# A hybrid encoder trunk on one core: four of the gate and branch blocks formed by seven half-size products in place of eight

## The chip, the cores and the metric

The kernel runs on one core of one Trainium2 chip. The metric is the device time of one execution in microseconds (us), input and output transfers of the launch left out. The engines are TensorE (PE in the profile, PEld its weight loads), VectorE (DVE), ScalarE (ACT), GpSimd (POOL) and SyncE (SP, here the queue that issues nearly all loads of weights).

## The reference

Two layers; all data are float32. SEQ is 256 rows (two row tiles of 128, called tt below), D is 1024. Each layer is a mixer and then a mixture of experts (MoE):

```python
h = modulate(rms_norm(x, norm1_g[i]), sh1, sc1)
proj = h @ w_in[i]                                   # (256,1024) @ (1024,6656)
u_hy, q, k, v, gate_hy, gate_at = jnp.split(proj, split_idx, axis=-1)
y_hy = hyena_mixer(u_hy, ...)                        # (256,768)
y_at = dilated_attention_mixer(rope(q), rope(k), v)  # (256,256)
merged = (sigmoid(gate_hy) * (y_hy @ w_br_h[i])      # (256,768) @ (768,1024)
          + sigmoid(gate_at) * (y_at @ w_br_a[i]))   # (256,256) @ (256,1024)
x = x + g1[:, None, :] * (merged @ w_out[i])
h = modulate(rms_norm(x, norm2_g[i]), sh2, sc2)
x = x + g2[:, None, :] * grouped_moe(h, ...)         # 16 experts, 3 matrices of 1024x512 each
```

gate_hy and gate_at are each 1024 columns of `proj`: four column blocks of W = 512, called gate blocks 0 to 3 here. `y_hy @ w_br_h` has two column blocks of 512, called branch blocks 0 and 1.

## The kernel before

All five engines have a program of their own, written out in order; semaphores (`p_...` counted by PE, `v_...` by DVE, `a_...` by ACT) are the only thing that orders one engine against another. PE's order in a layer is: projections of `h`, the convolution, attention (eight units, with gate blocks 0 and 1 woven in), then the stage that the change touches, the product with `w_out`, the router, and the MoE in seven steps.

The stage begins behind the last attention unit. `branch(q, w, src, ks, o)` forms one column block of a branch: for each row tile `ks` matmuls with 128 rows of `src` as weights and 512 columns of `w` moving, into bank 2 or 3. Branch blocks 0 and 1 take x0T (y_hy transposed, six chunks of 128 rows) and `w_br_h`. `gate(q, tt, half)` does the same for gate blocks from hT (eight chunks) and `w_in`, into bank 7 or 4; blocks 2 and 3 stand behind the branch blocks. Then `branch(2)` and `branch(3)` take the attention's part (two chunks). ACT opens the gates (Sigmoid, `open_gate`), DVE multiplies (L1868, L1871) and adds (L1872) into `merged`, whose transposes (L1083) PE does next.

In layer 0 DVE also forms, between its other work, the sums of the next layer's modulation: `next_sums(n, n+1)` is eight scaled additions `ada_part` of 512 columns each over a 2 MB block of `w_ada`, four blocks in all (L1586, L1588, L1590). `ada_post(n, L + 1)` on PE, eight instructions in the trace, folds each finished block and stands between the branch and gate blocks. In layer 1 there are none of these.

Weights pass through a ring of six buffers of 2 MB (two halves each) and, for the MoE, some further half buffers in idle memory: TABLE (in cst), EXTRA to EXTRA + 3 (in `wide`), ROWS and TAIL (in area). `place_blocks` plans the slots, `released` says which semaphore frees each, and SP issues the loads strictly in that order, so one load that waits for its slot holds all behind it. EXTRA to EXTRA + 2 lie where the convolution keeps its tables, and before the change are free once branch block 1 is done.

Of the kernel before, what the change touches and what calls it, by code (L numbers as in the profile page):

```python
# [14 lines left out]
P = 128  # L15
# [53 lines left out]
RING = 6  # L69
EXTRA = 2 * RING  # L70
# [114 lines left out]
def trunk_kernel(nc, t, out):  # L185
    with ExitStack() as ctx:
# [111 lines left out]
        mtmp = region(W)  # L298

# [97 lines left out]
        p_c = sem("p_c")  # L397
        v_c = sem("v_c")
        a_c = sem("a_c")
        p_vec = sem("p_vec")  # L400
        p_hv = sem("p_hv")
# [5 lines left out]
        v_A2 = sem("v_A2")  # L407
# [36 lines left out]
        p_br = sem("p_br")  # L444
        v_br = sem("v_br")
# [5 lines left out]
        p_sh = sem("p_sh")  # L451
# [6 lines left out]
        v_lg = sem("v_lg")  # L458
        a_xn = sem("a_xn")
        p_lg = sem("p_lg")  # L460
        a_lg = sem("a_lg")
        v_oh = sem("v_oh")
# [55 lines left out]
        def place_blocks():  # L518
            landings = [0] * len(halves)
            free = [(u, None) for u in range(EXTRA)]  # L520
            for key in loads:
                L, kind, b, half = key
                if kind == "moe":
                    if (b, half) == ((0, 0, 0), 0):
                        free = [(u, None) for u in (TABLE, EXTRA, EXTRA + 1, EXTRA + 2)]\
                            + [f for f in free if f[0] < EXTRA] + [(EXTRA + 3, None)]
                        if L + 1 == DEPTH:
                            free.insert(12, (ROWS, None))
# [24 lines left out]
        def released(L, kind, b, half):  # L553
# [5 lines left out]
            if kind == "in":  # L559
                if b < 4:  # L560
                    return p_u, L * NSC + 4 * b + 4
                if b < 7:
                    return p_qk, L * 6 + 2 * b - 7
                return (p_v, L * 3 + (1, 3)[b - 7]) if b < IN_A else (p_gate, L * 8 + 2 * (b - IN_A) + 2)
            if kind == "brh":
                return p_br, L * 8 + 2 * b + 2
            if kind == "bra":
                return p_br, L * 8 + 8
# [52 lines left out]
        def _(sp):  # L621
# [7 lines left out]
            for L, kind, b, half in loads:  # L629
                _, u, _, olds = plan[L, kind, b, half]  # L630
                dst, landing, _ = slot(L, kind, b, half)
                for old in olds:
# [3 lines left out]
                    elif u == TABLE:  # L636
                        sp.wait_ge(p_br, L * 8 + 1)
                    elif u == ROWS:
                        sp.wait_ge(p_br, L * 8 + 8)
# [40 lines left out]
        def _(pool):  # L680
# [15 lines left out]
            for L in range(DEPTH):  # L696
# [20 lines left out]
                if L + 1 < DEPTH:  # L717
                    pool.wait_ge(p_lg, L + 1)
# [14 lines left out]
        def _(pe):  # L733
# [11 lines left out]
            for L in range(DEPTH):  # L745
# [80 lines left out]
                if L == 0:  # L826
                    pe.wait_ge(s_id, 16)
                    pe.wait_ge(s_mlp, 16 * N_MLP)
                    pe.transpose(bank[4][:, 0:4], hrow, ident[0:4, 0:4]).then_inc(p_hv, 1)
# [4 lines left out]
                    pe.transpose(bank[0][:, 0:ND], crow, ident[0:ND, 0:ND]).then_inc(p_c, 1)  # L834
# [20 lines left out]
                    for l in range(DEPTH):  # L855
                        pe.transpose(bank[6][:, l * P:l * P + R_ALL], vrows[l][:, :], ident[0:R_ALL, 0:R_ALL])
                    pe.transpose(bank[6][:, DEPTH * P:DEPTH * P + DEPTH * 6 * ND], brow[:, :],
                                 ident[0:DEPTH * 6 * ND, 0:DEPTH * 6 * ND]).then_inc(p_vec, 1)
# [163 lines left out]
                def gate(q, tt, half):  # L1022
                    w = block_of("in", IN_A + q)
                    if q >= 1 and half == 0:
                        pe.wait_ge(a_gate, L * 8 + 2 * q + tt - 1)
# [14 lines left out]
                for u in range(UNITS):  # L1040
# [5 lines left out]
                    if u == 5:  # L1046
                        pe.wait_ge(v_sh, 2 * L + 2)
                        pe.wait_ge(v_mod, (L + 1) * 4)
                        mm(bank[1][:, 0:NE], ones, shift_sum, True, True).then_inc(p_sh, 1)
                if L + 1 < DEPTH:  # L1050
                    ada_post(0, L + 1)

                def branch(q, w, src, ks, o):
                    for tt in range(NT):
                        if q >= 1:
                            pe.wait_ge(v_br, L * 8 + 2 * q + tt - 1)
                        for k in range(ks):
                            last = mm(bank[2 + tt][:, :], src[:, k, tt * P:(tt + 1) * P], w[:, k, o:o + W],
# [3 lines left out]
                for q in range(2):  # L1062
                    wv = landed("brh", q)[:, 0:NH_CH * W].rearrange("p (k f) -> p k f", f=W)
                    branch(q, wv, x0T, NH_CH, 0)
                    if L + 1 < DEPTH:
                        ada_post(1 + q, L + 1)
                for q in (2, 3):
                    for tt in range(NT):
                        gate(q, tt, 0)
                        gate(q, tt, 1)  # L1070
                        if L + 1 < DEPTH and (q, tt) == (2, 1):
                            ada_post(3, L + 1)
                wv = landed("bra", 0)[:, 0:2 * D].rearrange("p (k f) -> p k f", f=D)
                pe.wait_ge(a_yat, L + 1)
                branch(2, wv, yatT, 2, 0)
                branch(3, wv, yatT, 2, W)
# [53 lines left out]
                last.then_inc(p_lg, 1)  # L1130
# [3 lines left out]
                pe.wait_ge(v_oh, L + 1)  # L1134
# [98 lines left out]
                pe.wait_ge(a_xn, L + 1)  # L1233
# [68 lines left out]
        def _(sc):  # L1302
# [7 lines left out]
            sc.wait_ge(p_c, 1)  # L1310
            sc.activation(stat[:, 0, 0:ND], bank[0][:, 0:ND], ACT.Sigmoid).then_inc(a_c, 1)

            for L in range(DEPTH):
# [68 lines left out]

                def open_gate(q, tt):
                    if q >= 2:
                        sc.wait_ge(v_br, L * 8 + 2 * (q - 2) + tt + 1)
                    sc.wait_ge(p_gate, L * 8 + 2 * q + tt + 1)
# [21 lines left out]
                for q in (2, 3):  # L1408
                    for tt in range(NT):
                        open_gate(q, tt)  # L1410
# [34 lines left out]
                sc.wait_ge(v_lg, L + 1)  # L1445
                sc.activation(rt[score], rt[logit], ACT.Sigmoid).then_inc(a_lg, 1)
# [4 lines left out]
                last.then_inc(a_xn, 1)  # L1451
# [91 lines left out]
        def _(dv):  # L1543
# [22 lines left out]
            for L in range(DEPTH):  # L1566
# [105 lines left out]
                if L == 0:  # L1672
                    dv.wait_ge(p_hv, 1)
# [16 lines left out]
                    dv.wait_ge(p_vec, 1)  # L1690
# [48 lines left out]
                def second_shift_and_scale():  # L1739
# [4 lines left out]
                    dv.scalar_tensor_tensor(A2[:, :], modT[:, 4 * ND:5 * ND], 1.0, n2[:, L, :],  # L1744
                                            ALU.add, ALU.mult).then_inc(v_A2, 1)
                    dv.wait_ge(v_A2, L + 1)
# [93 lines left out]
                ada_parts(N_LATE, 0, 2 * ND)  # L1840
                ada_gate(N_LATE)
                ada_gate(N_LATE + 1)

                def next_sums(first, stop):
                    for n in range(first, stop if L + 1 < DEPTH else first):
                        for k in range(ND):
                            ada_part(n, k, L + 1, "next")

                next_sums(0, 1)
                dv.wait_ge(p_sh, L + 1)  # L1850
                link(dv.tensor_copy(shift_logit, bank[1][:, 0:NE]))
                next_sums(1, 2)
                for q in range(4):
# [297 lines left out]
```

## Time and profile before

| | |
|---|---|
| three runs, median (lowest to highest) | 1084.14 us (1083.87 to 1084.25) |
| the profiled execution | 1084.34 us, span 1082.6 us |
| mean granted clock of PE | 0.994 |
| PE busy / PEld / DVE / ACT | 97% / 53% / 43% / 16% of the span |
| stage of the change, layer 0 | from 243.66 us of the span |
| stage of the change, layer 1 | from 758.98 us of the span |
| MoE, layer 0 / layer 1 | from 343.76 / 856.42 us |
| moved from memory | 332.78 MB, mean 307 GB/s |

The span runs from the first to the last instruction. A float32 matmul shows as two PE instructions in the trace and as one in the program order, so a count in the trace is twice the number of matmuls. A merged row of PE gives the start, the time to the modelled end of its last matmul (which overlaps the next row) and the count; the pace is read from start to start.

### The profile page before, as it was taken

The page shows a single profiled execution, that of the slowest core. Times are in us where ns is not written, and L with a number is a line of the kernel's source. Part 1 is how long each engine was busy: PE and PEld are TensorE (multiplying, and loading weights), DVE is VectorE, ACT ScalarE, POOL GpSimd, SP SyncE. Part 2 cuts the span into 40 slices and gives each one's busy share as a digit, 9 for nine tenths or more (in the row PEclk, how much of TensorE's full clock was granted, in tenths as well). Part 3 has the DMA queues.
Part 4 walks back from the last instruction along what each step waited for, and adds up shares of the span by engine and source line. Part 5 has one row for each costly group of instructions (what it writes and reads, how often), then busy time and mean ns, then how long its engine had stood idle before and what let it go on. Part 6 is the DMA issues. An engine that isn't in the chain of part 4 may idle for free.

```text
span 1082.6 us, 17591 instructions
## 1 busy us (share of the span) xinstructions
PE 1048.1 (97%) x7533; PEld 574.6 (53%) x7533; DVE 469.6 (43%) x1024; ACT 174.3 (16%) x340; POOL 20.4 (2%) x40
## 2 busy tenths in 40 slices
PE   7999999999999999999999999999999999999895
PEld 4788667654446344433448866765444634444231
DVE  3477696644125422351335779660102532222223
ACT  4121101310014113101121110031001411111002
POOL 3000000000000000000000000000000000000000
PEclk9999999999999999999999999999999999999898
DMA  9996846268963999999999884525665399999993
GB/s 314 391 386 250 305 157 212 82 215 320 414 233 133 407 420 413 423 420 420 421 400 377 301 299 169 181 94 194 245 266 226 127 420 423 420 421 420 421 421 135
DMA packets 90917, 332.78 MB, mean 307 GB/s; under 512 B 5020, under 2 KB 5355, under 8 KB 66005
## 3 DMA queue, kind: packets, MB, share of 16 engines
q1 hardware_dynamic: 87905, 323.56, 76.6%
q0 software_dynamic: 2048, 6.09, 1.6%
q10 hardware_dynamic: 884, 1.97, 0.6%
q8 instruction: 61, 1.00, 0.4%
q14 instruction: 19, 0.16, 0.0%
HBM read 330.54 MB, written 1.05 MB: 306 GB/s over the span
## 4 chain that ended last, share of the span: by engine, by line
PE 87%; DVE 6%; DMA 3%; SPq 1%; issue 1%; ACT 1%; DVEq 0%
PE bank L735 84%; DMA ring<-in_moe_w_dram 3%; SPq L665 1%; PE bank L1175 1%; PE bank L1007 1%; DVE wide L1588 0%; DVE area L1781 0%; DVE wide L1786 0%; DVE area L1784 0%; PE bank L1093 0%; DVE area L1782 0%; DVE area L1783 0%; PE bank L788 0%; DVE wide L1785 0%; DVE area L1659 0%
## 5 line engine op out<-in xcount | busy, mean ns | idle before, releaser
L735 PE MATMUL bank<-ring,hT 128*32 128x512 f32 (+3 forms) x1808 | 313.1, 557 | 1.7 <-issue 1.7
L735 PE MATMUL bank<-hT,ring 128*32 128x256 f32 (+1 forms) x2112 | 214.1, 380 | 0.2 <-DVE hT L1622 0.2
L735 PEld LDWEIGHTS bank<-ring,hT 128*32 128x32 f32 (+2 forms) x1808 | 128.8, 136 | 150.0 <-issue 146.3
L735 PEld LDWEIGHTS bank<-hT,ring 128*32 128x32 f32 (+1 forms) x2112 | 158.9, 132 | 55.1 <-issue 8.7
L735 PE MATMUL bank<-area 32*64 32x64 f32 (+5 forms) x648 | 96.1, 363 | 0.5 <-ACT area L1470 0.5
L735 PE MATMUL bank<-ring,area 128*32 128x512 f32 x664 | 81.9, 594 | 0.5 <-ACT area L1470 0.5
L735 PEld LDWEIGHTS bank<-area 32*64 32x64 f32 (+4 forms) x648 | 43.8, 145 | 54.2 <-issue 52.2
L2055 DVE TENSOR_TENSOR area<-bank,area 128x512 f32<-128x512 f32 x14 | 9.7, 692 | 130.2 <-PE bank L735 130.2
L735 PE MATMUL bank<-wide,hT 128*32 128x512 f32 x368 | 65.8, 603 | 0.0
L1588 DVE SCALAR_TENSOR_TENSOR area<-ring,wide,area 128x512 f32<-128x512 f32 x84 | 63.1, 751 | 2.5
L735 PE MATMUL bank<-ring,wide 128*128 128x512 f32 (+1 forms) x192 | 64.0, 597 | 0.0
L735 PE MATMUL bank<-ring,xn 128*128 128x512 f32 x128 | 55.6, 592 | 0.0
L2066 DVE TENSOR_TENSOR area<-bank,g2b 128x512 f32<-128x512 f32 x28 | 19.4, 692 | 79.2 <-PE bank L735 79.2
L735 PE MATMUL bank<-area,xn 128*128 128x128 f32 x448 | 52.5, 275 | 0.1
L735 PEld LDWEIGHTS bank<-area,xn 128*128 128x128 f32 x448 | 51.1, 192 | 0.4 <-issue 0.4
L1985 DVE TENSOR_TENSOR x<-x,bank 128x512 f32<-128x512 f32 x56 | 38.5, 688 | 24.8 <-PE bank L735 24.8
L735 PEld LDWEIGHTS bank<-ring,area 128*32 128x32 f32 x664 | 22.3, 110 | 44.1 <-issue 42.5
L735 PEld LDWEIGHTS bank<-ring,wide 128*128 128x128 f32 (+1 forms) x192 | 25.4, 163 | 33.6 <-issue 30.5
L1971 DVE TENSOR_SCALAR hT<-bank,A,modT 128x128 f32<-128x128 f32 x56 | 19.1, 404 | 52.2 <-PE bank L735 52.2
L735 PEld LDWEIGHTS bank<-ring,xn 128*128 128x128 f32 x128 | 24.0, 190 | 28.7 <-issue 28.7
L1464 ACT ACTIVATE area<-bank 128x512 f32<-128x512 f32 x14 | 8.4, 598 | 185.4 <-PE bank L735 185.4
L735 PE MATMUL bank<-cst,hT 128*32 128x512 f32 x128 | 34.2, 622 | 2.8 <-DMA wide<-in_moe_w_dram 2.8
(266 smaller groups left out, 898.0 us busy)
## 6 DMA issues: line engine op xcount, KB each, us to landing
ring<-in_moe_w_dram SPq DMA_DIRECT2D x135, 1024.0 KB, 14.4
ring<-in_w_in_dram SPq DMA_DIRECT2D x26, 2048.0 KB, 11.3
ring<-in_w_ada_dram SPq DMA_DIRECT2D x24, 2048.0 KB, 14.1
wide<-in_moe_w_dram SPq DMA_DIRECT2D x33, 1024.0 KB, 12.5
cst<-in_moe_w_dram SPq DMA_DIRECT2D x13, 1024.0 KB, 15.0
area<-in_moe_w_dram SPq DMA_DIRECT2D x11, 1024.0 KB, 14.6
ring<-in_w_out_dram SPq DMA_DIRECT2D x4, 2048.0 KB, 7.8
ring<-in_w_br_h_dram SPq DMA_DIRECT2D x4, 1536.0 KB, 7.8
```

Source lines behind the costliest of these rows:

```text
L665: sp.dma_start(dst.rearrange("p (k f) -> p k f", f=D if m == 2 else FE), t[name][L, experts[e], :, :].rearrange(order, p=P)[:, part, :]).t ...
L735: return pe.matmul(dst, lhsT, rhs, start=start, stop=stop, skip_group_check=True)
L1007: last = pe.transpose(bank[5][:, b * P:(b + 1) * P], prob[:, u, b * P:(b + 1) * P], ident)
L1175: last = pe.transpose(bank[0][:, f * P:(f + 1) * P], act[:, f::NF], ident)
L1464: sc.activation(sil, bank[0][:, :], ACT.Silu).then_inc(a_sil, 1)
L1588: link(dv.scalar_tensor_tensor(part, wk, c, part, ALU.mult, ALU.add))
L1971: last = dv.tensor_scalar(hg[:, k, :], bank[3][:, (k - 4) * P:(k - 3) * P], A2[:, k:k + 1], modT[:, 3 * ND + k:3 * ND + k + 1], ALU.mult, ...
L1985: dv.tensor_tensor(x[:, tt, cols], x[:, tt, cols], bank[2 + 2 * tt + h][:, :], ALU.add)\
L2055: dv.tensor_tensor(act, bank[1][:, :], sil, ALU.mult).then_inc(v_act, 1)
L2066: dv.tensor_tensor(yS[:, cols], bank[6 + h][:, :], g2b[:, cols], ALU.mult).then_inc(v_yS, 1)
```

## The change

Four blocks in each layer (branch blocks 0 and 1, gate blocks 2 and 3) are formed by `seven(...)` instead of `branch` and `gate`. The block's product (256 rows by 512 columns) is cut in two by two quarters of 128 rows by 256 columns, the inner dimension in two halves of `kc` chunks (3 or 4). The eight quarter products become seven (Strassen's scheme in Winograd's form): each is `kc` matmuls of 256 columns. Their operands are sums that DVE forms: `sum_of` (of x0T or hT, four for each pair of blocks, 384 or 512 columns), `mix` (of the weights, four for each block, 768 or 1024 columns, the third in place in the ring). The results are put together by ACT, which copies products 1 and 2 out (`keep_products`), and by DVE, which forms two partial sums (`first_sums`) and three quarters (`quarter`), each 256 columns, and in blocks 0 and 1 multiplies them with the gates (`merge`). In gate blocks 2 and 3 ACT applies Sigmoid by quarters (`open_quarters`).

Product 1 of a block waits for `quarter(1)` of the block before, product 3 for its `quarter(2)`; product 4 waits for ACT's copy of product 1, product 5 for the first partial sum, product 6 for ACT's second copy, product 7 for `quarter(0)` and the last `mix`.

DVE's order is written out by hand in `block_in_seven`; the 16 remaining additions for the next layer (layer 0 only) are strewn into the four blocks as 3, 2, 4 and 7. EXTRA + 2 now holds operands of the scheme, is free only when all 28 products of the layer are done, and is moved from the fourth to the tenth place of the first MoE loads. Some semaphores are joined to free others for this.

```diff
@@ PE
+                def seven(i, w, src, sums, mixed, kc):
+                    n = L * SEVEN + i
...
+                    if i:
+                        pe.wait_ge(v_sev, n * 4 - 1)
+                    if i > 2:
+                        pe.wait_ge(a_gate, L * 12 + 5)
+                    product(X, of(0, 0), whole(0, 0), True)
+                    pe.wait_ge(v_sum, L * 8 + i // 2 * 4 + 1)
+                    pe.wait_ge(v_mix, n * 4 + 1)
+                    product(Y, summed(0), combined(0), True)
+                    if i:
+                        pe.wait_ge(v_sev, n * 4)
+                    else:
+                        pe.wait_ge(a_gate, L * 12 + 3)
+                    pe.wait_ge(v_sum, L * 8 + i // 2 * 4 + 2)
+                    pe.wait_ge(v_mix, n * 4 + 2)
+                    product(V, summed(1), combined(1), True)
+                    pe.wait_ge(a_sev, n * 2 + 1)
+                    product(X, of(1, 0), whole(1, 0), False)
...
+                    pe.wait_ge(v_sev, n * 4 + 1)
+                    product(V, summed(2), whole(0, 1), False)
...
+                    pe.wait_ge(a_sev, n * 2 + 2)
+                    product(Y, summed(3), whole(1, 1), False)
+                    pe.wait_ge(v_mix, n * 4 + 4)
+                    pe.wait_ge(v_sev, n * 4 + 2)
+                    product(V, of(1, 1), combined(2), False)
@@ DVE
+                def block_in_seven(i, parts):
+                    at = [parts[0]]
+                    def fill(n):
+                        for _ in range(min(n, parts[1] - at[0])):
+                            next_part(at[0])
+                            at[0] += 1
+                    mix(i, 3)
+                    first_sums(i)
+                    if i == 2:
+                        sum_of(2, 3)
+                    if i < 3:
+                        mix(i + 1, 0)
+                    fill(1)
+                    quarter(i, 0)
+                    if i < 3:
+                        mix(i + 1, 1)
+                    fill(2)
+                    quarter(i, 1)
+                    if i < 3:
+                        mix(i + 1, 2)
+                    if i == 1:
+                        sum_of(2, 2)
+                    fill(2)
+                    quarter(i, 2)
+                    fill(ND)
...
+                block_in_seven(0, (2 * ND, 2 * ND + 3))
+                block_in_seven(1, (2 * ND + 3, 2 * ND + 5))
+                block_in_seven(2, (2 * ND + 5, 3 * ND + 1))
+                block_in_seven(3, (3 * ND + 1, 4 * ND))
@@ SP
+                    elif u == EXTRA + 2:
+                        sp.wait_ge(p_sev, (L + 1) * SEVEN * 7)
                     elif u >= EXTRA:
-                        sp.wait_ge(p_br, L * 8 + 4)
+                        sp.wait_ge(p_sev, (L * SEVEN + 2) * 7)
```

PE, layer 0, the start of the stage (`ring` are the weights as loaded, `wide` before the change is x0T, 128x1 is `ada_post`). Before:

```order
L735 MATMUL bank<-cst,area 128x1 x4
L735 MATMUL bank<-ring,wide 128x512 x12
L735 MATMUL bank<-cst,area 128x1 x4
L735 MATMUL bank<-ring,wide 128x512 x12
L735 MATMUL bank<-cst,area 128x1 x4
L735 MATMUL bank<-ring,hT 128x512 x16
```

And with the change, where the rows that name `wide` alone take combined operands on both sides:

```order
L756 MATMUL bank<-cst,area 128x1 x4
L756 MATMUL bank<-ring,wide 128x256 x3
L756 MATMUL bank<-wide 128x256 x6
L756 MATMUL bank<-ring,wide 128x256 x9
L756 MATMUL bank<-wide 128x256 x3
L756 MATMUL bank<-cst,area 128x1 x4
L756 MATMUL bank<-ring,wide 128x256 x3
```

Each block of twelve matmuls of 512 columns is now 21 of 256; one `ada_post` is still between blocks 0 and 1, and the one that stood between blocks 1 and 2 now stands behind block 3.

DVE, layer 0, around branch block 0 (`xn` holds the opened gates). Before, from the last addition ahead of the block:

```order
L1590 SCALAR_TENSOR_TENSOR area<-ring,wide,area 128x512
L1868 TENSOR_TENSOR area<-bank,xn 128x512 x2
L1586 TENSOR_SCALAR area<-ring,wide 128x512
L1588 SCALAR_TENSOR_TENSOR area<-ring,wide,area 128x512 x6
L1590 SCALAR_TENSOR_TENSOR area<-ring,wide,area 128x512
```

With the change, from `quarter(0, 0)` to `quarter(0, 2)` (the three rows of L1991; product 1 of block 1 waits for the second of them):

```order
L1991 TENSOR_TENSOR area<-bank,area 128x256
L1983 TENSOR_TENSOR area<-area,xn 128x256
L1983 TENSOR_TENSOR area<-bank,xn 128x256
L1969 TENSOR_TENSOR wide<-ring,wide 128x768
L1674 SCALAR_TENSOR_TENSOR area<-ring,wide,area 128x512 x2
L1991 TENSOR_TENSOR area<-bank,area 128x256
L1983 TENSOR_TENSOR area<-area,xn 128x256
L1969 TENSOR_TENSOR ring<-ring 128x3x256
L1991 TENSOR_TENSOR area<-bank,area 128x256
```

Between the first quarter and the second stand two gate products, a combination of block 1's weights and two additions for the next layer.

## Rows read from the trace of the kernel before

**Rows 1.** The page, busy time, share of the span and instructions by engine.

```profile
PE 1048.1 (97%) x7533; PEld 574.6 (53%) x7533; DVE 469.6 (43%) x1024; ACT 174.3 (16%) x340; POOL 20.4 (2%) x40
```

**Rows 2.** Timeline of PE, layer 0, the stage of the change: start, us, instructions.

```profile
243.66 10.55 PE L735 MATMUL bank<-ring,wide 128*128 128x512 f32 x24
254.04 0.95 PE L735 MATMUL bank<-cst,area 128*128 128x1 f32 x8
254.85 10.55 PE L735 MATMUL bank<-ring,wide 128*128 128x512 f32 x24
...
266.04 13.98 PE L735 MATMUL bank<-ring,hT 128*128 128x512 f32 x32
...
294.49 7.19 PE L735 MATMUL bank<-ring,wide 128*128 128x512 f32 x16
```

**Rows 3.** Timeline of PE, layer 1, the same stage.

```profile
758.98 20.87 PE L735 MATMUL bank<-ring,wide 128*128 128x512 f32 x48
779.68 27.63 PE L735 MATMUL bank<-ring,hT 128*128 128x512 f32 x64
```

**Rows 4.** Timeline of PE, layer 1, projections: matmuls of 256 columns in four waited groups.

```profile
603.95 13.98 PE L735 MATMUL bank<-hT,ring 128*128 128x256 f32 x64
617.77 1.02 PE L735 MATMUL bank<-area,cst 128*128 128x512 f32 x2
```

**Rows 5.** Groups by line and shape, DVE, 60 to 1075 us: count, busy us, mean ns.

```profile
L1588 DVE SCALAR_TENSOR_TENSOR area<-ring,wide,area 128x512 f32<-128x512 f32 x84 | 63.1, 751 | 2.5
L1872 DVE TENSOR_TENSOR area<-area 128x512 f32<-128x512 f32 x8 | 5.5, 692 | 0.3
L1659 DVE TENSOR_TENSOR wide<-wide 128x1536 f32<-128x1536 f32 x2 | 3.5, 1756 | 0.0
```

**Rows 6.** Timeline of DVE, layer 0, around branch block 0.

```profile
235.91 4.69 DVE L1588 SCALAR_TENSOR_TENSOR area<-ring,wide,area 128x512 f32<-128x512 f32 x6
240.64 0.75 DVE L1590 SCALAR_TENSOR_TENSOR area<-ring,wide,area 128x512 f32<-128x512 f32 x1
249.16 0.69 DVE L1868 TENSOR_TENSOR area<-bank,xn 128x512 f32<-128x512 f32 x1 [7.77 <-PE bank L735]
254.31 0.69 DVE L1868 TENSOR_TENSOR area<-bank,xn 128x512 f32<-128x512 f32 x1 [4.46 <-PE bank L735]
254.92 0.48 DVE L1586 TENSOR_SCALAR area<-ring,wide 128x512 f32<-128x512 f32 x1
```

**Rows 7.** The chain that ended last, layer 0, behind the stage.

```profile
302.54 0.70 DVE area L1872
303.29 1.09 PE bank L1083 x8
```

**Rows 8.** The page, weight loads of 128 columns: count, busy us, mean ns.

```profile
L735 PEld LDWEIGHTS bank<-ring,xn 128*128 128x128 f32 x128 | 24.0, 190 | 28.7 <-issue 28.7
```

**Rows 9.** Timeline of SP's queue, layer 0.

```profile
266.47 3.31 SPq L665 DMA_DIRECT2D cst<-in_moe_w_dram  x1
```

**Rows 10.** Stretches of layer 1 by engine; the last three numbers are PEclk, DMA share, GB/s.

```profile
855.00:860.00 5.00, 4.96 (x44) 4.79 (x43) 1.56 (x6) 1.68 (x5) 0.00 (x0) 1.00 0.01 3
865.00:870.00 5.00, 5.00 (x52) 1.46 (x48) 4.31 (x21) 0.60 (x1) 0.00 (x0) 1.00 0.92 370
```

**Rows 11.** The chain that ended last, layer 1, MoE.

```profile
990.32 27.67 DMA ring<-in_moe_w_dram
```

**Rows 12.** Timeline of PE, layer 1, MoE: in brackets the idle time before.

```profile
1010.67 0.62 PE L735 MATMUL bank<-cst,hT 128*32 128x512 f32 x2 [2.77 <-DMA wide<-in_moe_w_dram]
...
1043.42 3.64 PE L735 MATMUL bank<-ring,hT 128*32 128x512 f32 x32 [1.66 <-issue]
```

**Rows 13.** Stretches by engine around these two waits, columns as in rows 10.

```profile
1009.30:1012.70 3.40, 2.03 (x16) 0.72 (x20) 0.00 (x0) 0.00 (x0) 0.00 (x0) 0.80 1.02 424
1012.70:1016.00 3.30, 3.30 (x24) 0.84 (x16) 0.00 (x0) 0.00 (x0) 0.00 (x0) 0.69 1.00 415
...
1041.00:1044.00 3.00, 1.34 (x16) 0.33 (x12) 0.00 (x0) 0.00 (x0) 0.00 (x0) 1.00 1.01 421
```

More of the change, by code:

```diff
@@ L69 @@
 RING = 6
+SEVEN = 4
+HW = W // 2
 EXTRA = 2 * RING
@@ L1063, in _ @@
                     wv = landed("brh", q)[:, 0:NH_CH * W].rearrange("p (k f) -> p k f", f=W)
-                    branch(q, wv, x0T, NH_CH, 0)
-                    if L + 1 < DEPTH:
-                        ada_post(1 + q, L + 1)
+                    seven(q, wv, x0T, sums_x, mixed_h, half_h)
+                    if L + 1 < DEPTH and q == 0:
+                        ada_post(1, L + 1)
                 for q in (2, 3):
[L1068 to L1072, printed above, removed]
+                    seven(q, block_of("in", IN_A + q), hT, sums_h, mixed_d, half_d)
+                if L + 1 < DEPTH:
+                    ada_post(2, L + 1)
                 wv = landed("bra", 0)[:, 0:2 * D].rearrange("p (k f) -> p k f", f=D)
@@ L1075, in _ @@
                 branch(2, wv, yatT, 2, 0)
+                if L + 1 < DEPTH:
+                    ada_post(3, L + 1)
                 branch(3, wv, yatT, 2, W)
@@ L1407, in _ @@
                 last.then_inc(a_yat, 1)
-                for q in (2, 3):
-                    for tt in range(NT):
-                        open_gate(q, tt)
+                for i in range(SEVEN):
+                    keep_products(i)
+                    if i >= 2:
+                        open_quarters(i)
                 for j in range(4):
@@ L1450, in _ @@
                                          scale=rs[:, tt:tt + 1])
-                last.then_inc(a_xn, 1)
+                last.then_inc(a_score_xn, 1)
                 def rows_to_h():
@@ L1840, in _, with next_part, next_sums, operands @@
                 ada_parts(N_LATE, 0, 2 * ND)
+                def next_part(i):
+                    if L + 1 < DEPTH:
+                        ada_part(i // ND, i % ND, L + 1, "next")
+                def next_sums(n):
+                    for k in range(ND):
+                        next_part(n * ND + k)
+                def operands(i):
+                    if i < 2:
+                        return x0T, sums_x, mixed_h, half_h, "brh", i
+                    return hT, sums_h, mixed_d, half_d, "in", IN_A + i
@@ new lines, in sum_of @@
+                def sum_of(i, j):
+                    src, sums, _, kc, _, _ = operands(i)
+                    lo, hi = slice(0, kc), slice(kc, 2 * kc)
+                    a11, a12, a21, a22 = (src[:, h, tt * P:(tt + 1) * P] for tt in range(NT) for h in (lo, hi))
+                    a, b, op = ((a21, a22, ALU.add), (sums[0], a11, ALU.subtract), (a11, a21, ALU.subtract),
+                                (a12, sums[1], ALU.subtract))[j]
+                    if j in (1, 3):
+                        dv.wait_ge(v_sum, L * 8 + i // 2 * 4 + j)
+                    dv.tensor_tensor(sums[j], a, b, op).then_inc(v_sum, 1)
@@ L1841, in _ @@
+                for j in range(4):
+                    sum_of(0, j)
                 ada_gate(N_LATE)
+                for j in range(2):
+                    sum_of(2, j)
                 ada_gate(N_LATE + 1)
[L1844 to L1850, printed above, removed]
@@ L1851, in _ @@
[L1851 to L1862 removed]
+                next_sums(0)
```

210 lines of the change are left out of this document (147 added, 63 removed).

## The prediction

> **What bounds the kernel now.** I read the busy shares first: PE is busy for 97% of the span [rows 1]. Then PE's timeline in the two stretches that the change touches. In layer 0 the two branch blocks take 10.38 us each (243.66 to 254.04), the two gate blocks 13.82 us each, with 0.81 us of `ada_post` between them (254.04 to 254.85), and no row has idle time before it [rows 2]. In layer 1 the branch pair runs from 758.98 to 779.68 with nothing between [rows 3]. So here PE's own instructions set the time, at 10.38 / 24 = 0.4325 us for each instruction of 512 columns. Last, DVE in layer 0: it finished the second block of additions at 241.4, then sat idle 7.8 us until the first half of branch block 0 was there, and 4.5 us until the second [rows 6]. There is room on DVE, but in pieces.
>
> **What is removed.** 2 x 10.38 + 2 x 13.82 = 48.4 us of matmuls in each layer become seven eighths of that, if a matmul of 256 columns costs half of one of 512. It does: 64 instructions of 256 columns in four groups, each of which waits for a semaphore, take 13.82 us from start to start, 0.216 us each [rows 4]. A product is 6 instructions (1.30 us) in the branch blocks and 8 (1.73 us) in the gate blocks, a block 9.07 or 12.10 us. Removed: 6.05 us in each layer, 12.1 us in all.
>
> **What DVE adds.** A TENSOR_TENSOR takes 0.692 us for 512 columns and 1.756 for 1536, both operands in SBUF [rows 5]: 1.04 ns a column, so 0.43 us for 256, 0.96 for 768 and 1.22 for 1024. Where the next instruction waits for the result its start comes 0.04 us behind the end (six linked additions, 235.91 to 240.64, 0.79 each for a duration of 0.75 [rows 5, 6]); where it doesn't wait it comes 0.08 us ahead of the end (254.31 to 254.92 for 0.69 [rows 6]). From PE's last matmul to DVE: 243.66 + 12 x 0.4325 = 248.85, and DVE starts at 249.16, so 0.31 us [rows 2, 6]. From DVE's end to PE: 302.54 + 0.69 to 303.29, 0.06 us [rows 7]. The sums of x0T and hT, and the first three combinations for block 0 (241.4 to 244.3), fit the idle time that DVE had ahead of and in block 0; the combination that product 2 needs is done at 242.4, when product 1 has not begun. They cost nothing. Without that cover they would be some 2 us in each layer.
>
> **Where PE must wait.** The tight place is the border between two blocks. Product 1 of the next block waits for `quarter(1)`, and DVE gets to that only when it has done, behind product 5, `quarter(0)`, its two gate products (branch blocks), one combination for the next block and up to two additions for the next layer. Counted from the start of a block:
> - Layer 0, block 0: product 5 ends at 5 x 1.296 = 6.48, DVE starts `quarter(0)` at 6.79. Then 0.47 (quarter, waited for), 0.35 + 0.35 (gate products), 0.88 (768 columns), 2 x 0.79 (additions), 0.43 (`quarter(1)`) and 0.06 to PE: 10.91. PE is there at 9.07 + 0.81 of `ada_post` = 9.88 and waits 1.0 us.
> - Layer 0, block 1: DVE comes 0.16 late to `quarter(0)` (3 x 1.296 + 0.31 = 4.20, then 0.35 + 0.47 for the first sums, 1.14 for 1024 columns, 0.79: 6.95). 6.95 + 0.47 + 0.70 + 1.14 + 0.79 + 0.43 + 0.06 = 10.54, against 9.07 with no `ada_post` behind: 1.5 us.
> - Layer 0, block 2: 5 x 1.73 + 0.31 = 8.95, then 0.35 + 1.14 + 0.79 + 0.67 + 0.43 + 0.06 = 12.39, against 12.10: 0.3 us.
> - Layer 1 has no additions: block 0 gives 9.33 against 9.07, 0.3 us; block 1 gives 9.59 against 9.07, 0.5 us; block 2 10.93 against 12.10, none.
>
> Together 3.6 us. Within a block the waits hold less: product 5 needs the first partial sum 1.30 us after product 3's end, and 0.31 + 0.43 + 0.06 = 0.80 us do; product 7 needs the same after product 5. ACT's copies have more than a product's time. Behind block 3 DVE has seven additions (5.5 us) in 12.1 us of PE, and the last of them is wanted only by `ada_post(3)` behind `branch(2)`.
>
> At the five waits PE must restart. From nothing (the weight load done during the wait) to a whole load of 0.19 us [rows 8]; I take 0.1 each, 0.5 us. For the 56 borders between products whose semaphores have long come I take nothing, since the four groups of rows 4 show none at their borders; the upper bound is again a load not hidden, 0.19 us.
>
> **The loads.** SP's order changes little. In layer 0 the first MoE load was issued at 266.47 [rows 9]. Now the second `w_out` block ahead of it takes the slot of the third block of additions, of which the last is now in block 2, about 277. All 18 half blocks that the slots hold still have some 60 us to come in before the MoE; 20 MB need 48 us at 420 GB/s. EXTRA + 2 is free later, but stands later in the order. In layer 1 DMA stood still at 855 to 860 and ran at 370 GB/s from 865 [rows 10]: every slot was full when the MoE began, and its loads are released by the MoE's own matmuls. So the MoE and its loads move forward together, and the gain of the stage should reach the end.
>
> **The sum.** 12.1 - 3.6 - 0.5 = 8.0 us. From the profiled execution's 1084.34 us that is 1076.3; the median of the runs shown is 0.2 us below that execution, so **1076.1 us**. By layer: some 3.0 us in layer 0 and 5.0 in layer 1.
>
> **Rivals.**
> - *DVE never holds PE* (0.08). For it: DVE is 43% busy [rows 1]. Against: the count above. Gain 12.1, 1072.0 us.
> - *DVE holds PE longer* (0.13): some of the new instructions, whose operands lie in pieces in the ring or are in place, cost more than 1.04 ns a column, or every start is a waited one. At 0.12 us more for each DVE instruction between the quarters, the five waits grow by about 0.5 each and block 2 of layer 1 stays free: gain 5.5; at 1.3 ns a column the same count gives about 3.5. 1078.6 to 1080.6 us.
> - *The clock falls* (0.07). After a wait of 2.77 us PE's granted clock was 0.80 and then 0.69 in the next two stretches, (0.20 x 3.4 + 0.31 x 3.3) = 1.7 us lost at the lower level, 1.2 GHz; after one of 1.66 us it stayed at 1.00 [rows 12, 13]. My waits are 1.5 us at most. If the three of layer 0 each cost one such fall: 5.1 us less, 1081.2. The Trainium skill has a rule that speaks for this ("TensorE: Matmul & The Clock Gate", section "A second HAM failure mode: psum-queue depth-cycling"): short idle times between groups of matmuls, when they are frequent, let the clock swing between its two levels. The row with 1.66 us speaks against it here.
> - *The loads hold layer 1* (0.07). The chain has one wait of 27.67 us for a MoE load there [rows 11]. If the last loads land when they did, layer 1's 5.0 us are lost and only layer 0's 3.0 stay: 1081.2. Against it: the idle DMA ahead of the MoE [rows 10].
> - *Every product pays its border* (0.06, the side of slower). If the semaphore ahead of each product keeps its first weight load from lying under the matmul before it, 56 x 0.19 = 10.6 us [rows 8] come back: 12.1 - 3.6 - 10.6 = 2.1 us slower, 1086.2. It decides from 8.5 / 56 = 0.15 us a border. Against it stand the four waited groups of rows 4, but their semaphores came early, and the products' come within a microsecond.
>
> **How the numbers follow.** The count above has 0.59; its own range is 1074.5 to 1078.5. To hold 8 in 10 I take in most of the second rival and part of the first: 1073 to 1081. A measurement of this kernel can tell some 0.2% (2.2 us) from no change. All cases but the last lie beyond that on the fast side (0.94); for mixtures and for what I haven't seen I take off 0.06: faster 0.88, same 0.06, slower 0.06.
>
> **What would show it.** In the profile after: branch block 0 in 9.1 us of PE, with 0.216 us an instruction; PE idle before the first product of blocks 1, 2 and 3 of layer 0 and released by the line of `quarter`, 1.0, 1.5 and 0.3 us; in layer 1 0.3, 0.5 and none; granted clock 1.00 in both stages; the MoE about 3 us earlier in layer 0 and 8 us in layer 1, with the same waits for loads at its end. I am wrong if idle time lies inside the blocks (ACT's copies or the partial sums), if the pace at 256 columns isn't 0.216, or if PE waits longer for loads in the MoE of layer 1.

## The result, and the profile after

| | before | after |
|---|---|---|
| median of the runs, us | 1084.15 (1083.87 to 1084.25) | 1077.87 (1077.67 to 1078.26) |
| profiled execution, us | 1084.34 | 1078.26 |
| its span, us | 1082.6 | 1076.4 |

The ratio is 0.994, with a 95% interval of 0.9928 to 0.9952: 6.3 us faster. The forecast was 1076.1 us with a range of 1073 to 1081, so 8.0 us were forecast. Run again beside the experiments the change took 1077.71 us against 1084.55, 6.8 us.

The page of the kernel after, busy time by engine, answers to [rows 1]: PE has 9.4 us less to do, DVE 57.8 us more.

```profile
PE 1038.7 (97%) x7701; PEld 606.3 (56%) x7701; DVE 527.4 (49%) x1120; ACT 182.1 (17%) x364; POOL 19.9 (2%) x40
```

The timeline of PE in layer 0's stage, after, answers to [rows 2]: start, us, instructions, and in brackets the idle time before the row and what ended it.

```profile
244.49 1.54 PE L756 MATMUL bank<-ring,wide 128*128 128x256 f32 x6
245.87 2.75 PE L756 MATMUL bank<-wide 128*128 128x256 f32 x12
248.46 4.05 PE L756 MATMUL bank<-ring,wide 128*128 128x256 f32 x18
252.34 1.46 PE L756 MATMUL bank<-wide 128*128 128x256 f32 x6
253.63 0.95 PE L756 MATMUL bank<-cst,area 128*128 128x1 f32 x8
255.44 1.53 PE L756 MATMUL bank<-ring,wide 128*128 128x256 f32 x6 [0.86 <-DVE area L1991]
...
266.00 1.97 PE L756 MATMUL bank<-ring,hT 128*128 128x256 f32 x8 [1.26 <-DVE area L1991]
...
278.40 1.96 PE L756 MATMUL bank<-ring,hT 128*128 128x256 f32 x8
...
290.57 0.95 PE L756 MATMUL bank<-cst,area 128*128 128x1 f32 x8
...
299.22 1.04 PE L1152 MATMUL bank<-cst,area 128*128 128x128 f32 x8
```

Line 756 is the helper that issues every matmul, 1991 the addition in `quarter`, 1152 the transposes behind the stage. Block 0 is 42 instructions from 244.49 to 253.63, 9.14 us: no idle time lies inside it, and its products follow each other at 0.216 us an instruction, but for the first, whose six take 1.38 us where 1.30 would be that pace. The idle time is where blocks meet. The distances from one block's first product to the next one's are 10.95, 10.56 and 12.40 us.

The timeline of PE in layer 1's stage, after, answers to [rows 3].

```profile
758.02 1.56 PE L756 MATMUL bank<-ring,wide 128*128 128x256 f32 x6
...
767.36 1.53 PE L756 MATMUL bank<-ring,wide 128*128 128x256 f32 x6
...
776.94 1.97 PE L756 MATMUL bank<-ring,hT 128*128 128x256 f32 x8 [0.28 <-DVE area L1991]
...
789.10 1.89 PE L756 MATMUL bank<-ring,hT 128*128 128x256 f32 x8
...
801.19 4.16 PE L756 MATMUL bank<-ring,wide 128*128 128x512 f32 x9
```

Here they are 9.34, 9.58, 12.16 and 12.09 us (the last row goes on beyond the window that was asked for). Small waits show only in such distances: between 758.02 and 767.36 no row has a bracket, yet 9.34 is 0.27 more than 42 instructions take at 0.216 us; the slower first product accounts for about 0.1 of it.

The timeline of DVE, after, from the first half of block 0 to the first product of block 1, answers to [rows 6].

```profile
251.30 0.42 DVE L1991 TENSOR_TENSOR area<-bank,area 128x256 f32<-128x256 f32 x1 [0.43 <-DVE area L1672]
251.76 0.42 DVE L1983 TENSOR_TENSOR area<-area,xn 128x256 f32<-128x256 f32 x1
252.10 0.42 DVE L1983 TENSOR_TENSOR area<-bank,xn 128x256 f32<-128x256 f32 x1
252.44 0.95 DVE L1969 TENSOR_TENSOR wide<-ring,wide 128x768 f32<-128x768 f32 x1
253.30 1.53 DVE L1674 SCALAR_TENSOR_TENSOR area<-ring,wide,area 128x512 f32<-128x512 f32 x2
254.87 0.42 DVE L1991 TENSOR_TENSOR area<-bank,area 128x256 f32<-128x256 f32 x1
```

This is `quarter(0)`, its two gate products, a combination for the next block, two of the next layer's additions, and `quarter(1)`, on which PE's product at 255.44 waits. The prices are those that were forecast (0.42 for 0.43, 0.95 for 0.96), in the ring and in place as well.

The windows of the two stages, after, answer to [rows 10, 13] for the clock (columns as there): both at PEclk 1.00, that is at 2.4 GHz. In the first window DVE is busy for 43.25 us of 57, with the scheme's work, the gate products and the 16 additions together.

```profile
243.00:300.00 57.00, 54.81 (x260) 45.11 (x258) 43.25 (x69) 8.06 (x20) 0.00 (x0) 1.00 0.84 313
755.00:810.00 55.00, 53.98 (x235) 42.29 (x233) 30.52 (x50) 9.11 (x21) 0.00 (x0) 1.00 0.72 270
```

**Where the rest of the gain went.** PE's timeline cut at the same rows in each trace gives, in us: A, from the start of the span to the first matmul group `bank<-area,wide` of 384 columns; B, layer 0's stage, from its first product to the transposes behind it; C, layer 0's experts (MoE) to the transposes with which layer 1 begins; D, layer 1's stage; E, from the start of layer 1's MoE to the end. Between these pieces all traces agree within some 0.1 us, but for one that is told of below.

```
                      A       B       C       D       E     span
before              20.68   57.85  222.88   55.19  226.18  1082.6
after               21.52   54.73  224.23   50.20  225.93  1076.4
a_after             20.11   54.73  224.57   50.19  226.40  1075.8
e_quarters_first    20.35   55.12  224.35   49.43  226.05  1075.1
e_extra_fourth      21.56   54.73  222.87   50.20  226.24  1075.4
e_fewer_additions   21.22   52.90  224.28   50.20  226.18  1074.6
b_spread            21.45   51.94  224.50   49.43  225.85  1073.0
b_spread_fourth     21.50   51.93  222.87   49.43  226.15  1071.7
p_before_tenth      20.81   57.86  232.17   55.19  226.05  1093.1
```

The two stages gain 3.12 and 4.99 us, 8.1 together. C gives back 1.35 and A 0.84; E gains 0.25, and 6.2 us are left. A varies between 20.11 and 21.52 in two executions of the same kernel, ahead of everything that was changed: it is chance. C is longer in both, by 1.35 and 1.69 us: that comes from the change. The timeline of PE at the end of layer 0's MoE, after, shows it; before has no wait there.

```profile
552.95 0.62 PE L756 MATMUL bank<-ring,area 128*32 128x512 f32 x2 [0.89 <-DMA area<-in_moe_w_dram]
```

### The profile page after: what moved, and what is told of

It reads as the page before. It is cut to its first block, busy times and chain, and to the rows that moved or that the text cites. A ratio compares the mean times of both kernels' runs of the same rounds, so it can differ in the third digit from the quotient of the medians.

```text
span 1076.4 us, 18126 instructions
## 1 busy us (share of the span) xinstructions
PE 1038.7 (97%) x7701; PEld 606.3 (56%) x7701; DVE 527.4 (49%) x1120; ACT 182.1 (17%) x364; POOL 19.9 (2%) x40
## 4 chain that ended last, share of the span: by engine, by line
PE 84%; DVE 7%; DMA 5%; issue 1%; SPq 1%; ACT 1%; DVEq 0%
PE bank L756 81%; DMA ring<-in_moe_w_dram 3%; DMA area<-in_moe_w_dram 2%; SPq L686 1%; PE bank L1028 1%; PE bank L1244 1%; DVE wide L1674 0%; DVE area L1866 0%; DVE wide L1871 0%; DVE area L1869 0%; PE bank L1162 0%; DVE area L1868 0%; DVE area L1867 0%; PE bank L809 0%; DVE wide L1870 0%
## 5 line engine op out<-in xcount | busy, mean ns | idle before, releaser
L756 PE MATMUL bank<-ring,hT 128*32 128x512 f32 (+3 forms) x1808 | 283.4, 551 | 4.9 <-DMA ring<-in_moe_w_dram 2.1
L756 PEld LDWEIGHTS bank<-ring,hT 128*32 128x32 f32 (+2 forms) x1808 | 120.2, 134 | 135.2 <-issue 129.9
L756 PE MATMUL bank<-ring,area 128*32 128x512 f32 (+1 forms) x680 | 103.5, 584 | 1.8 <-ACT area L1556 0.9
L756 PE MATMUL bank<-wide,hT 128*32 128x512 f32 (+1 forms) x376 | 76.8, 584 | 0.0
L756 PEld LDWEIGHTS bank<-ring,area 128*32 128x32 f32 (+1 forms) x680 | 31.6, 113 | 52.8 <-issue 49.5
L756 PE MATMUL bank<-ring,wide 128*128 128x256 f32 (+2 forms) x224 | 52.2, 475 | 0.9 <-DVE area L1991 0.9
L756 PEld LDWEIGHTS bank<-ring,wide 128*128 128x128 f32 (+1 forms) x224 | 31.4, 167 | 14.8 <-issue 10.2
L756 PEld LDWEIGHTS bank<-wide,hT 128*32 128x32 f32 (+1 forms) x376 | 24.1, 118 | 27.2 <-issue 26.4
```

The source lines that it names most:

```text
L756: return pe.matmul(dst, lhsT, rhs, start=start, stop=stop, skip_group_check=True)
```

## The experiments

The kernel before ran on the same chip beside each of the two sets of experiments, at 1084.55 us (1083.55 to 1085.01) beside the first four below and 1084.59 (1084.01 to 1085.05) beside the last three. Theory: DVE's work ahead of `quarter(1)` sets the waits at the borders, and the place of EXTRA + 2 in the order of slots sets the wait in layer 0's MoE. Rivals: the borders cost something of their own (banks, ScalarE's copies, a restart of PE), and the loads as a whole are the bound in layer 0's MoE.

**The change again (a_after).**

> The changed kernel itself, as the yardstick on this chip for the three beside it. In the trace of the change the two stages were 3.1 us (layer 0) and 5.0 us (layer 1) shorter, 8.1 together, but the whole only 6.2. Theory: 0.8 us of the difference is the start of the program, where PE's clock rose 1.7 us later than in the profile of before, and is chance; 1.3 us is the MoE of layer 0, where PE waits 0.9 us for a load, and is a result of the change. If so this run shows the wait of layer 0's MoE again (0.9 us), and the start at either value. Rival: both are chance; then the wait comes and goes, and the median lies up to 2 us lower.

Measured: 1077.71 us (1077.46 to 1078.62), ratio 0.994 [0.9927, 0.9952]. B, D and the waits in them repeat to 0.01 us; A doesn't. The wait for a load in layer 0's MoE is there again, 1.37 us in place of 0.89, so the rival, that both are chance, is out; the size of the wait isn't fixed.

**Quarters first (e_quarters_first).**

```diff
                     quarter(i, 0)
-                    if i < 3:
-                        mix(i + 1, 1)
-                    fill(2)
                     quarter(i, 1)
                     if i < 3:
+                        mix(i + 1, 1)
                         mix(i + 1, 2)
+                    quarter(i, 2)
                     if i == 1:
                         sum_of(2, 2)
-                    fill(2)
-                    quarter(i, 2)
                     fill(ND)
```

> The change, with DVE's order altered only: quarter(1) directly behind quarter(0), the two combinations for the next block behind it, then quarter(2) and the additions. Nothing is taken out or added. Theory: PE's waits ahead of blocks 1 to 3 (0.86, 1.26, 0.28 us in layer 0, 0.28 in layer 1) are a matter of what stands ahead of quarter(1); by the count of the prediction it would be done 8.6 us after a block's start, ahead of the 9.07 at which PE is there, so all four waits go: some 2.5 us faster than the change, a few tenths less if DVE then comes late to quarter(2). Rival: DVE's load in layer 0 as a whole is too large (some 9.6 us for a block of 9.9 or 9.1), then the waits only move to product 3 or 7 of the next block and the time stays within 0.5 us.

Measured: 1076.51 us (1075.6 to 1076.94), ratio 0.9925 [0.9912, 0.9938]. That is 1.2 us less than the change beside it, where 2.5 were expected. All border waits went. Layer 1's stage takes 49.43 us. Layer 0's takes 55.12, more than the change's own, for a reason that PE's timeline of this kernel shows (its stage begins at 243.30):

```profile
286.58 0.95 PE L756 MATMUL bank<-cst,area 128*128 128x1 f32 x8
287.39 3.68 PE L756 MATMUL bank<-ring,wide 128*128 128x512 f32 x8
291.86 1.05 PE L756 MATMUL bank<-cst,area 128*128 128x1 f32 x8 [0.79 <-DVE area L1676]
293.19 5.40 PE L756 MATMUL bank<-ring,wide 128*128 128x512 f32 x8 [0.28 <-DVE area L2049]
```

Block 3 ends at 286.58, 43.28 us behind the start of the stage; in the change it is 46.08, so 2.80 us were gained up to there. But the edit also leaves all additions but one of each block for the end, and six were still to be made then; `ada_post(3)` waits for the last of them, `branch(3)` for a merge that stands behind them on DVE. The eight matmuls at 293.19 (`branch(3)`) took 5.40 us where eight of the same shape at 287.39 (`branch(2)`) took 3.68. The windows of this kernel (columns as before) say why:

```profile
290.00:292.00 2.00, 1.21 (x5) 0.33 (x3) 1.93 (x4) 0.00 (x0) 0.00 (x0) 1.00 0.98 410
292.00:296.00 4.00, 3.73 (x13) 2.10 (x14) 2.48 (x4) 0.00 (x0) 0.00 (x0) 0.76 1.02 426
296.00:300.00 4.00, 3.46 (x13) 1.70 (x11) 2.62 (x4) 0.94 (x2) 0.00 (x0) 0.81 1.02 424
```

The granted clock fell to its lower level, 1.2 GHz, for part of the two last windows. Behind waits of 1.1 us by the brackets (1.5 by subtracting starts) that cost some 1.7 us more. It is seen in this one trace: over the whole span the mean granted clock was 0.991 in the profiled execution and 0.995 in three of the other four, so it need not come every time.

**EXTRA + 2 back to the fourth place (e_extra_fourth).** The change, but with the old order of slots:

```diff
-                        ringed = [f for f in free if f[0] < EXTRA]
-                        free = [(u, None) for u in (TABLE, EXTRA, EXTRA + 1)]\
-                            + ringed[:RING] + [(EXTRA + 2, None)] + ringed[RING:] + [(EXTRA + 3, None)]
+                        free = [(u, None) for u in (TABLE, EXTRA, EXTRA + 1, EXTRA + 2)]\
+                            + [f for f in free if f[0] < EXTRA] + [(EXTRA + 3, None)]
```

> The change, with EXTRA + 2 back in the fourth place of the first MoE loads, as before the change, though it is free only after all products. Theory A (the slots): in layer 0 the tenth place makes its second turn fall on load 28, in a step where it may not be used, so that it is lost there and not at load 40, and with it a buffer; then the wait of 0.9 us in the MoE of layer 0 is gone here, and the time is 0.9 us shorter. Theory B (the start of the loads): the loads of the MoE start later than before the change; here they start later still (about 290 and not 278 us), so the wait stays or grows, by up to a few us. Neither expects a change in the stage.

Measured: 1076.92 us (1075.71 to 1077.65), ratio 0.9928 [0.9915, 0.9941]. That is 0.8 us less than a_after's median, as theory A has it, but the ranges of the two overlap; C tells more. It is 222.87 us, that of before, and the waits of PE in it, by line and releaser (total, times, longest), no longer hold a load:

```profile
PE bank L1243 <- DVE area L2239: 1.8, 2, 0.9
PE bank L755 <- ACT area L1555: 0.5, 1, 0.5
PE bank L755 <- DVE wide L1737: 0.4, 1, 0.4
```

SP's row with the three loads into `wide` is now 12.05 us long, since the third of them, the fourth load in all, waits for all 28 products. That cost nothing: the load that fills the last slot ahead of the MoE is issued at 331.97 us, in the change at 331.92. What the tenth place costs comes 250 us later. A slot is struck off the list when its turn comes for a step behind the one that the table `LAST` gives it, step 1 for EXTRA + 2 in layer 0. Counted through `place_blocks`, from the fourth place it takes the loads of index 3 (step 0) and 20 (step 1) and then goes; from the tenth it takes load 9, and its next turn is load 28, of step 2, so it goes after one. It serves one load less, and the loads behind it come one slot later. In layer 0 e_extra_fourth has the plan of the kernel before, and the kernel of the next experiment has the plan of the change.

**That order of slots alone (p_before_tenth).** The kernel before with EXTRA + 2 in the tenth place, and its load waiting for the gates:

```diff
-                        free = [(u, None) for u in (TABLE, EXTRA, EXTRA + 1, EXTRA + 2)]\
-                            + [f for f in free if f[0] < EXTRA] + [(EXTRA + 3, None)]
+                        ringed = [f for f in free if f[0] < EXTRA]
+                        free = [(u, None) for u in (TABLE, EXTRA, EXTRA + 1)]\
+                            + ringed[:RING] + [(EXTRA + 2, None)] + ringed[RING:] + [(EXTRA + 3, None)]
...
+                    elif u == EXTRA + 2:
+                        sp.wait_ge(p_gate, L * 8 + 8)
```

> The kernel before the change, with one part of it: EXTRA + 2 moved to the tenth place of the first MoE loads, where it waits for the last gate block. Theory A (the slots): PE waits some 0.9 us for a load in the MoE of layer 0, and the time is 0.9 us longer than before. Theory B (the start of the loads): nothing changes, since the first loads start as before.

Measured: 1092.04 us (1087.29 to 1094.88), ratio 1.0056 [1.0039, 1.0072]: slower, by 2.7 to 10.3 us in its six runs, and C is 9.3 us longer. The sign is that of the theory, the size isn't. The timeline of PE at the end of layer 0's MoE in this kernel:

```profile
546.84 3.64 PE L738 MATMUL bank<-ring,hT 128*32 128x512 f32 x32 [0.50 <-DMA ring<-in_moe_w_dram]
...
556.83 0.62 PE L738 MATMUL bank<-ring,area 128*32 128x512 f32 x2 [0.40 <-DMA area<-in_moe_w_dram]
...
568.65 8.79 PE L738 MATMUL bank<-cst 128*128 128x256 f32 x28 [4.53 <-issue]
```

Only 0.9 us are waits for loads, about as in the change. Most of the rest is a hole of 4.53 us, which ended with nothing that the profile shows, and the lower clock behind it (28 matmuls in 8.79 us; 5.79 in before, at 561.02, with no hole): 7.5 of this execution's 9.3 us. In the code nothing stands between the MoE and these 28 matmuls but the reading of a flag, which DVE had set at 357 us, and the branch on it around the rare case of too many tokens. The profile has a packet of the queue of kind "instruction" between 565 and 570 us and none between 552 and 565, where before has one in each of 552 to 560 and 560 to 565. That code arrived late behind the loads would fit, but the change has no hole there, and its own packet of that kind falls in 560 to 565 too, with the 28 matmuls begun at 560.07; no run here tests it. (This trace also lost 1.2 us to a wait for a load ahead of B.)

**Fewer additions (e_fewer_additions).**

```diff
-                block_in_seven(0, (2 * ND, 2 * ND + 3))
-                block_in_seven(1, (2 * ND + 3, 2 * ND + 5))
+                block_in_seven(0, (2 * ND, 2 * ND))
+                block_in_seven(1, (2 * ND + 3, 2 * ND + 3))
```

> The changed kernel without the five parts of the next layer's gate sums that VectorE adds in blocks 0 and 1 of layer 0 (they are left out, so layer 1's third gate row is not the reference's; blocks 2 and 3 keep theirs). If these additions (0.74 us each) are what makes the two border waits of layer 0 larger than layer 1's, the waits before blocks 1 and 2 fall from 0.86 and 1.26 us to layer 1's: none and 0.28 us, and the stage of layer 0 takes 54.73 - 0.86 - 0.98 = 52.9 us. The wait of 0.25 us before block 3 stays. If VectorE's waits at a border are the sum of something else (the wait for the bank, ScalarE's copies), the two waits stay near 0.9 and 1.3 us and the stage at 54.7. Loads at the end of layer 0's experts should then give back up to 1.8 us of the gain, since they come no earlier: median 1076 to 1077.5 us by the first theory, 1077.7 by the second.

This kernel leaves out five of the next layer's additions, so its result isn't the reference's; only its times are used. Measured: 1075.87 us (1075.57 to 1076.41), ratio 0.9921 [0.9907, 0.9934]; layer 0's stage 52.90 us, as expected. The timeline of PE in layer 0's stage, this kernel:

```profile
254.17 1.54 PE L756 MATMUL bank<-ring,wide 128*128 128x256 f32 x6
...
263.76 1.97 PE L756 MATMUL bank<-ring,hT 128*128 128x256 f32 x8 [0.28 <-DVE area L1991]
...
276.30 1.97 PE L756 MATMUL bank<-ring,hT 128*128 128x256 f32 x8 [0.21 <-issue]
```

So the additions, and nothing else, make layer 0's first two borders longer than layer 1's. C stays at 224.28: the stage came out 1.83 us shorter, and none of that was lost to the loads. The expectation that they would give back up to 1.8 us failed, and the median lies just below its range.

**Both repairs (b_spread, b_spread_fourth).** Quarters first as above, with the additions put into DVE's holes in blocks 2 and 3, and the second kernel with the fourth place as well:

```diff
-                    fill(1)
+                    fill((1, 1, 1, 3)[i])
                     quarter(i, 0)
+                    fill(i // 2)
                     quarter(i, 1)
                     if i < 3:
                         mix(i + 1, 1)
                         mix(i + 1, 2)
+                    fill(i // 3)
                     quarter(i, 2)
...
-                block_in_seven(2, (2 * ND + 5, 3 * ND + 1))
-                block_in_seven(3, (3 * ND + 1, 4 * ND))
+                block_in_seven(2, (2 * ND + 5, 3 * ND + 2))
+                block_in_seven(3, (3 * ND + 2, 4 * ND))
```

> The quarters of a block ahead of the mixes of the next, as in the run before, and the next layer's additions brought into the holes that VectorE has in blocks 2 and 3 (3 of them before the first quarter of block 3, one each between its quarters, one more in block 2), so that one instead of five is left when the last product ends. Nothing is left out. If the 0.79 and 0.28 us waits after the last block, and the fall of the clock behind them, came from the late additions alone, the waits go, the clock stays at full speed, and the stage of layer 0 takes 49.2 + 3.3 = about 52.4 us in place of 55.1 and 54.7; layer 1's stays at 49.4. If the fall of the clock has another cause (the sparse one column products there), it stays and the stage is near 54. With EXTRA + 2 in the tenth place the end of layer 0's experts waits for a load: it gives back 1 to 3 us of the 2.3, so 1074.5 to 1076.5 us; I take 1075.5.

> The same with the slot EXTRA + 2 back in the fourth place of the order in which layer 0's experts fill their slots. If that place alone is what lets a load of the last expert come late, the experts of layer 0 take 222.9 us and the whole gain of the stage reaches the end: 1 to 2 us faster than the kernel before it in this call, 1073.5 to 1075 us; I take 1074.3. If the loads as a whole are the bound by now (the engines move 420 GB/s through the experts and the stage is 5.5 us shorter than before the change), the experts of layer 0 take longer by what the stage gained, and it comes out at 1075.5 to 1076.5.

Measured: b_spread 1074.51 us (1074.07 to 1074.85), ratio 0.9908 [0.9892, 0.9923]; b_spread_fourth 1072.88 us (1072.19 to 1073.55), ratio 0.9892 [0.9877, 0.9907]. The timeline of PE in layer 0's stage, b_spread_fourth:

```profile
244.47 1.54 PE L755 MATMUL bank<-ring,wide 128*128 128x256 f32 x6
...
254.43 1.54 PE L755 MATMUL bank<-ring,wide 128*128 128x256 f32 x6
...
263.57 1.89 PE L755 MATMUL bank<-ring,hT 128*128 128x256 f32 x8
...
275.66 1.89 PE L755 MATMUL bank<-ring,hT 128*128 128x256 f32 x8
...
292.88 3.68 PE L755 MATMUL bank<-ring,wide 128*128 128x512 f32 x8
296.40 1.04 PE L1151 MATMUL bank<-cst,area 128*128 128x128 f32 x8
```

No wait is left in it, and the eight matmuls at 292.88 take 3.68 us again: with the waits the fall of the clock went too. Layer 0's stage came out 0.5 us shorter than expected (51.93 us), layer 1's as expected. b_spread's median is 1.0 us below the value expected, at the edge of its range; b_spread_fourth's is 1.4 us below and outside its range, since here too the loads took nothing back. The place of the slot is worth 1.6 us on both sides (1.63 in the medians, 1.63 in C), and the total is 11.7 us less than the kernel before.

## Why the prediction was right, and where it was off

**What bounds, and the product.** Right. The stage is PE's, and a product of 256-column matmuls costs half: 9.14 us for block 0 against 9.07. With every wait gone the stages are 5.92 and 5.76 us shorter than before, where 6.05 each were forecast: 0.4 us too much in all. Part of it is that layer 1's stage had been 0.25 us quicker in before than its 112 instructions at 0.4325 us (20.70 + 27.47 us up to the last two branches, not 48.4), which the forecast passed over.

**The borders.** Right. Forecast distances 10.91, 10.54 and 12.39 us, measured 10.95, 10.56 and 12.40; in layer 1 9.33, 9.59 and 12.10, measured 9.34, 9.58 and 12.16. e_fewer_additions shows which part is the additions', b_spread that the order on DVE is the whole cause. A count along DVE's order, with one price for an instruction that is waited for and one for one that isn't, came out to 0.06 us.

**The restart.** Mis-sized: 0.5 us taken, while the measured distances exceed the forecast ones by 0.13 us in all, and with the waits gone the stages are 3.57 us shorter (2.80 and 0.77), the same as the 3.6 that the forecast had for the waits without a restart. A restart is there: the first product behind a wait takes 1.37 us where one that was not waited for takes 1.29 (b_spread_fourth, layer 1, 763.04 to 764.33), and it begins 0.15 us behind DVE's end and not 0.06. But DVE's chain came out shorter by nearly as much, 3.57 us from `quarter(0)` to `quarter(1)` in block 0 of layer 0 where 3.63 were counted. Two errors cancelled, by luck: 0.4 us too much for the products, 0.5 too much for the restart, so that 8.0 was forecast for the stages and 8.1 measured.

**Borders between products.** Right: nothing. In b_spread_fourth's layer 0 block 2 is 12.09 us from its first product to block 3's, 56 instructions at 0.216. The rival that had every product pay its border is out.

**Sums and combinations ahead of block 0.** Right: PE waits for none of them, and DVE stood idle 2.67 us before the first sums.

**The clock.** No fall in the change: 1.00 in both stages, with waits of 0.86 and 1.26 us. But e_quarters_first shows that the rival can't be dismissed: waits of 0.79 and 0.28 us around a short group of one column matmuls were followed by the lower level, once. The length of the single wait doesn't order these cases, nor [rows 12, 13], where 1.66 us did no harm. The Trainium skill tells of short and frequent idle times between groups of matmuls behind which the clock swings ("TensorE: Matmul & The Clock Gate", section "A second HAM failure mode: psum-queue depth-cycling"). This trace agrees as far as it has two short waits close together, with 0.76 and 0.81 behind them; that their being repeated is what counts, no run here shows.

**"The gain of the stage should reach the end."** This is the step that failed, in part. I wrote of EXTRA + 2 that it "is free later, but stands later in the order", and looked at its first load alone, for which that is true. Its later turns decide: the tenth place takes one of them away, and in both executions of the change layer 0's MoE is longer, by 1.35 and 1.69 us. C is 224.23 to 224.57 us in all five traces with the tenth place behind a shortened stage, and 222.87 in both with the fourth. e_extra_fourth changes nothing else, so it is shown, and the rival "the loads as a whole are the bound" is out for layer 0. The signs named for it came out smaller too: the MoE begins 2.30 us earlier in layer 0 and 5.95 in layer 1, where 3 and 8 were forecast; the later start of the program took 0.84 off both, and C 1.35 more off the second. The count of the slots was off by one: 17 half blocks are issued ahead of layer 0's MoE, not 18; nothing hung on it. In layer 1 nothing was lost: E is the same within 0.3 us, though its MoE starts 6 us earlier, so the rival by which its loads hold it is out. The remaining 0.8 us of the difference in the profiled pair is the start of the program, chance.

## What to carry to other kernels

Halving a matmul's columns cost TensorE nothing here (0.216 us an instruction for 0.4325); what decided was the engine that makes the operands, and there not its busy share (49%) but its order. So put first what the next product waits for, and put filler work where that engine is idle anyway, but not all at the end, or the next consumer waits. Where a list gives out slots in turn, a place in it is not one event but a series of turns; follow it to its last one before calling a move free. And small waits have no bracket in a timeline: subtract starts.

## What was unexpected in the hardware

- In one trace a group of eight 512-column matmuls took 5.40 us in place of 3.68 after two waits of 0.79 and 0.28 us, while single waits of 0.86 and 1.26 us in front of 42 to 56 dense matmuls left the clock at 1.00.
- The order of slots that costs 1.35 us in the change costs 7.5 us (median) in the kernel before, and 9.3 in the profiled execution, of which 4.53 are a hole at a branch in PE's program, while DMA ran at full share, and 3.0 the lower clock behind it. What PE waited for stays open.
- Two executions of the same program differ by 1.4 us in their first 20 us. In a_after eight 256-column matmuls at 11.24 us took 1.99 us; in the profiled execution of the change the same eight, at 11.70, took 3.78, which is the pace of the lower level, so the clock had risen later. The windows do not show it, they give 1.00 for both; but the first entry of the granted clock in the two traces lies at 9.1 and at 16.4 us of the span. The difference is larger than most effects in this study, and it is why stages are compared here and not spans.
